# In the first block's two mixers, the z projection is put behind the values' projection inside the attention

## Chip, cores and metric

One core of one Trainium2 chip. The metric is device time in microseconds of one execution; the figure for the kernel before is the median of three runs. TensorE is PE here (its weight loads PEld), VectorE is DVE, ScalarE is ACT, GpSimd is POOL, and SyncE is SP, which issues the weight DMAs.

## What is computed

A sequence of 256 tokens of width 1024 goes through two blocks of two layers each, in fp32. A layer of the first block is a SwiGLU feed-forward, a hybrid mixer, and another feed-forward, each with a layer norm. Only the hybrid mixer matters here:

```python
def hybrid_mixer(x, w_in, b_in, ...):
    proj = x @ w_in + b_in
    (qa, ka, va, beta_raw, a_raw, za, qb, kb, vb, qc, kc, vc) = jnp.split(proj, split_at, axis=-1)
    o_a = gated_deltanet(qa, ka, va, beta_raw, a_raw, za, conv_w, a_log, dt_bias, gdn_norm_g)
    o_b = chunk_relpos_attention(qb, kb, vb, rel_bias)
    o_c = swa_sink_attention(qc, kc, vc, sinks)
    gates = jax.nn.sigmoid(x @ w_gate + b_gate).reshape(b, t, N_BRANCH, d)
    merged = (gates[:, :, 0] * (o_a @ w_br_a) + gates[:, :, 1] * (o_b @ w_br_b)
              + gates[:, :, 2] * (o_c @ w_br_c))
    return merged @ w_out

def gated_deltanet(qa, ka, va, beta_raw, a_raw, za, conv_w, a_log, dt_bias, norm_g):
    qkv = jax.nn.silu(causal_depthwise_conv(jnp.concatenate([qa, ka, va], -1), conv_w))
    ...
    beta = jax.nn.sigmoid(beta_raw)
    g = -jnp.exp(a_log) * jax.nn.softplus(a_raw + dt_bias)
    o = chunk_gated_delta_rule(q, k, v, g, beta)
    return o * lax.rsqrt(jnp.mean(o * o, -1, keepdims=True) + NORM_EPS) * norm_g * jax.nn.silu(z)
```

## The kernel before

**Products.** Every fp32 product is made of three matmuls on rounded parts: high times high, high times low, low times high (`mm3`, L444). The weights come from HBM in units of two k-tiles by 512 columns (SP, L2165). ACT rounds a unit to its high part (L922, "cut"), DVE subtracts to get its low part (L1266). Five units are cut ahead of their use.

**Order.** The order of all work is written out by one `Walk` that is replayed once per engine, so each engine runs its instructions in the order in which the Python code comes to them. Two things set it around the change. First, `attend` (L2518) advances nine attention items, one stage each, and after each round calls `fill(1)`. Second, `fill` (in `mixer1`) advances one generator of matrix work by one step of 12 small or 6 wide matmuls, and at every second step (at every step once the attention is over) pops one entry of a list `todo` of DVE and ACT work.

**The generator inside the attention** is `inputs_a`. It runs four parts of eight steps: the queries' columns (part 0), the keys' (part 1), then the part `None`, then the values' (part 2). Parts 0 to 2 write four PSUM banks of 256 columns each, which ACT empties (`conv_in`, L1015). The part `None` projects the delta rule's z together with beta and the decay inputs. It also uses four banks, DVE empties them in six instructions (`z_inputs`, L1399, L1400, L1402), and it appends four entries to `todo`: `decays_begin` (DVE L1460 to L1468, ACT L997), `decays_exp` (ACT L1004), `decays_log` (DVE L1475 to L1483), `decays` (DVE L1490 to L1501). These are 19 instructions on 8 columns each. Banks are handed out in the order in which they were given back (`bank`, L2290; `drop`, L2295).

**Behind the attention**, `gated()` is appended to `todo`: the convolution taps of the values (12 times DVE L1513), the silus of queries, keys and values (ACT L1028), the silu of z (ACT L1009). The generator becomes `others`: gate projection and branch output of the branches b and c, then the gate of a. After the eighth step of a gate projection DVE adds its bias (`gate`, L1679) and ACT takes the sigmoid (L1088). Once `todo` is empty, `delta` begins: its first matmuls are `gate_sums` (L607 to L611), `gd_rows` (L620), `gd_products` (L641) and `gd_turn` (L629). DVE's L1520 and ACT's L1033 empty the bank of `gate_sums`. DVE's L1587 gives LL, which PE needs at L651. `delta` is a long chain between PE, DVE, ACT and POOL, with `fill(2)` to `fill(4)` between its links:

```python
        state["every"] = 1
        todo.extend(gated())
        while not state["spent"]:
            fill(1)
...
        state["gen"], state["spent"] = others(), False
        fill(1)
        while todo:
            fill(1)
        ot = {}
        self.delta(l, fill, ot, done["b"] + done["c"])
```

Of the kernel before, what the change touches and what calls it, by code (L numbers as in the profile page):

```python
# [2221 lines left out]
class Walk:  # L2222
# [384 lines left out]
    def mixer1(self, l):  # L2607
# [36 lines left out]
        def convolve(j):  # L2644

            if j % 4 < 3:
                e.conv_first(l, j + 1)
            e.conv_taps(l, j)
# [5 lines left out]
                    lambda: e.conv_silu(l, 2), lambda: (e.z_gate(l, 0), e.z_gate(l, 1))]  # L2654

        def inputs_a():
            for part in (0, 1, None, 2):
                if part is None:
                    b0, b1 = [self.bank(), self.bank()], [self.bank(), self.bank()]
                    yield from self.rows(w_in, 8, 1536, [(0, 264, b0), (264, 256, b1)], self.x)  # L2660
                    for t in range(2):
                        e.z_inputs(l, t, b0[t], b1[t])
                        self.drop(b1[t], ("proj_v", (l, "z", t)))
                        self.drop(b0[t], ("proj_v", (l, "ba", t)))
                    todo.extend([lambda: e.decays_begin(l), lambda: e.decays_exp(l), lambda: e.decays_log(l), lambda: e.decays(l)])
                    continue
                bks = [self.bank() for _ in range(4)]
                yield from self.cols(w_in, 512 * part, 4, bks, self.x, steps=2)
                for j in range(4 * part, 4 * part + 4):
                    e.conv_in(l, j, bks[j % 4])  # L2670
                    self.drop(bks[j % 4], ("proj_a", (l, "q", j)))
                    if j % 4 == 1:
                        self.ahead(LEAD + 1)
                    if part < 2:
                        todo.append(lambda j=j: convolve(j))
                e.conv_first(l, 4 * part)

        state = {"gen": inputs_a(), "spent": False, "steps": 0, "every": 2}

        def fill(n):  # L2680
# [597 lines left out]
```

## Time and profile before

| | us |
|---|---|
| median of 3 runs | 2331.77 (2331.31 to 2331.85) |
| the profiled execution's own time | 2332.83 |
| its span in the trace | 2331.0 |
| PE busy | 2276.2 (98%) |
| DVE busy | 1485.0 (64%) |
| ACT busy | 1165.1 (50%) |
| POOL busy | 129.1 (6%) |
| granted PE clock, mean | 0.991 |

The two mixers of this kind run from about 320 to 565 us and from about 1165 to 1410 us of the span. A row of the timeline gives start, duration, engine, line, operation, output and inputs, and in brackets the idle time of the engine just before, with what ended it. Matmuls overlap, so a row's duration is longer than the distance to the next one.

### The profile page before, as it was taken

The page shows a single profiled execution, that of the slowest core. Times are in us where ns is not written, and L with a number is a line of the kernel's source. Part 1 is how long each engine was busy: PE and PEld are TensorE (multiplying, and loading weights), DVE is VectorE, ACT ScalarE, POOL GpSimd, SP SyncE. Part 2 cuts the span into 40 slices and gives each one's busy share as a digit, 9 for nine tenths or more (in the row PEclk, how much of TensorE's full clock was granted, in tenths as well). Part 3 has the DMA queues.
Part 4 walks back from the last instruction along what each step waited for, and adds up shares of the span by engine and source line. Part 5 has one row for each costly group of instructions (what it writes and reads, how often), then busy time and mean ns, then how long its engine had stood idle before and what let it go on. Part 6 is the DMA issues. An engine that isn't in the chain of part 4 may idle for free.

```text
span 2331.0 us, 33504 instructions
## 1 busy us (share of the span) xinstructions
PE 2276.2 (98%) x13839; PEld 1927.5 (83%) x13839; DVE 1485.0 (64%) x2139; ACT 1165.1 (50%) x1799; POOL 129.1 (6%) x197
## 2 busy tenths in 40 slices
PE   8999999999999999999999999999989999888999
PEld 7888798887888878888898877888878887766887
DVE  5665567857666556665667667666467664665663
ACT  5554346534555435553356344555344553545552
POOL 2100010120000000000100210000000000320000
PEclk9999999999999999999999999999999999999999
DMA  7856473445566556566553446566535665542663
GB/s 226 230 183 216 145 228 115 132 128 189 181 189 190 186 187 200 187 200 199 180 155 120 145 133 211 182 194 209 191 127 185 191 205 165 161 126 87 203 192 133
DMA packets 283560, 408.09 MB, mean 175 GB/s; under 512 B 13700, under 2 KB 170688, under 8 KB 283152
## 3 DMA queue, kind: packets, MB, share of 16 engines
q1 hardware_dynamic: 275600, 380.91, 51.4%
q0 software_dynamic: 7808, 25.04, 3.8%
q8 instruction: 109, 1.79, 0.3%
q14 instruction: 43, 0.35, 0.1%
HBM read 403.98 MB, written 1.91 MB: 174 GB/s over the span
## 4 chain that ended last, share of the span: by engine, by line
PE 85%; DVE 8%; ACT 4%; issue 1%; DMA 1%; POOL 0%; SPq 0%; DVEq 0%; ACTq 0%; POOLq 0%
PE PS L517 23%; PE PS L449 13%; PE PS L451 13%; PE PS L450 12%; PE PS L516 10%; DVE WL L1266 2%; PE PS L446 2%; PE PS L448 2%; PE PS L447 2%; PE PS L519 2%; PE PS L466 1%; ACT WH L922 1%; DVE QX L1513 1%; PE PS L661 0%; PE PS L677 0%
## 5 line engine op out<-in xcount | busy, mean ns | idle before, releaser
L1266 DVE TENSOR_TENSOR WL<-RW,WH 128x1024 fp32r<-128x1024 f32 (+2 forms) x732 | 870.8, 1220 | 315.8 <-ACT WH L922 312.2
L922 ACT ACTIVATE WH<-RW 128x1024 fp32r<-128x1024 f32 (+2 forms) x732 | 740.6, 1043 | 393.3 <-PE PS L451 220.9
L517 PE MATMUL PS<-XT,WH 128*128 128x512 f32 x2368 | 808.3, 394 | 0.0
L516 PE MATMUL PS<-XT,WL 128*128 128x256 f32 x2072 | 580.5, 280 | 0.0
L517 PEld LDWEIGHTS PS<-XT,WH 128*128 128x128 f32 x2368 | 425.0, 188 | 76.7
L516 PEld LDWEIGHTS PS<-XT,WL 128*128 128x128 f32 x2072 | 389.9, 188 | 13.3
L449 PE MATMUL PS<-WH,HTH 128*128 128x512 f32 x688 | 271.4, 394 | 0.0
L451 PE MATMUL PS<-WH,HTL 128*128 128x512 f32 x688 | 270.8, 394 | 0.0
L450 PE MATMUL PS<-WL,HTH 128*128 128x512 f32 x688 | 269.7, 392 | 0.0
L449 PE MATMUL PS<-WH,XT 128*128 128x512 f32 (+4 forms) x640 | 253.2, 396 | 8.0 <-DVE SX L1420 3.3
L451 PE MATMUL PS<-WH,XT 128*128 128x512 f32 (+4 forms) x640 | 243.0, 380 | 0.0
L450 PE MATMUL PS<-WL,XT 128*128 128x512 f32 (+4 forms) x640 | 242.5, 379 | 0.0
L446 PE MATMUL PS<-XT,WH 128*128 128x256 f32 x560 | 163.4, 292 | 2.4 <-DVE Z L1400 1.3
L449 PEld LDWEIGHTS PS<-WH,XT 128*128 128x128 f32 x640 | 123.7, 193 | 42.6 <-issue 9.9
L447 PE MATMUL PS<-XT,WL 128*128 128x256 f32 x560 | 157.6, 281 | 0.0
L448 PE MATMUL PS<-XT,WH 128*128 128x256 f32 x560 | 157.5, 281 | 0.0
L451 PEld LDWEIGHTS PS<-WH,HTL 128*128 128x128 f32 x688 | 129.1, 188 | 30.7
L1336 DVE TENSOR_TENSOR HM<-PS,HM 128x256 f32<-128x256 f32 x148 | 62.3, 421 | 144.3 <-ACT HM L952 144.3
L450 PEld LDWEIGHTS PS<-WL,HTH 128*128 128x128 f32 x688 | 129.1, 188 | 30.2
L449 PEld LDWEIGHTS PS<-WH,HTH 128*128 128x128 f32 x688 | 129.2, 188 | 28.9
L952 ACT ACTIVATE HM<-PS 128x256 f32<-128x256 f32 x148 | 57.0, 385 | 178.2 <-PE PS L517 174.0
L952 ACT ACTIVATE SG<-PS 128x256 f32<-128x256 f32 x148 | 57.1, 386 | 175.3 <-PE PS L517 174.6
(438 smaller groups left out, 2553.5 us busy)
## 6 DMA issues: line engine op xcount, KB each, us to landing
RW<-in_w_ff_in SPq DMA_DIRECT2D x256, 512.0 KB, 4.5
RW<-in_w_ff_out SPq DMA_DIRECT2D x128, 512.0 KB, 4.5
RW<-in_w_in SPq DMA_DIRECT2D x56, 512.0 KB, 4.5
RW<-in_w_gate SPq DMA_DIRECT2D x48, 512.0 KB, 4.3
RW<-in_ffn_gate SPq DMA_DIRECT2D x44, 512.0 KB, 4.6
RW<-in_ffn_up SPq DMA_DIRECT2D x44, 512.0 KB, 4.7
RW<-in_ffn_down SPq DMA_DIRECT2D x44, 512.0 KB, 4.5
RW<-in_w_out SPq DMA_DIRECT2D x16, 512.0 KB, 4.8
```

What stands on the lines that cost most here:

```text
L446: self.e.matmul(o, wh, xh, start=start, stop=False)
L447: self.e.matmul(o, wl, xh, start=False, stop=False)
L448: return self.e.matmul(o, wh, xl, start=False, stop=stop)
L449: self.e.matmul(o, xh, wh, start=start, stop=False)
L450: self.e.matmul(o, xh, wl, start=False, stop=False)
L451: return self.e.matmul(o, xl, wh, start=False, stop=stop)
L516: self.e.matmul(k.PS[:, b.n, 0:T], wl, k.XTH[:, kt, :], start=False, stop=False)
L517: ins = self.e.matmul(k.PS[:, b.n, :], wh, k.XT[:, kt, :], start=kt == 0, stop=kt == 7)
L922: self.e.activation(u.hi_out, raw, ACT.Copy).then_inc(*self.s["hi"].up(u.n))
L952: self.e.activation(f[2 + part][:, n, j * T:j * T + T], self.k.PS[:, b.n, 0:T], ACT.Copy).then_inc(*self.s["ffn_a"].up((seq, sl, n, part, j)))
L1266: self.e.tensor_tensor(u.lo_out, raw, u.hi_out.bitcast(F), ALU.subtract).then_inc(*self.s["lo"].up(u.n))
L1336: self.e.tensor_tensor(v, self.k.PS[:, b.n, T:2 * T], v, ALU.add).then_inc(*self.s["ffn_v"].up((seq, sl, n, part, j)))
```

## The change

One tuple is reordered, in `mixer1`:

```diff
         def inputs_a():
-            for part in (0, 1, None, 2):
+            for part in (0, 1, 2, None):
                 if part is None:
                     b0, b1 = [self.bank(), self.bank()], [self.bank(), self.bank()]
                     yield from self.rows(w_in, 8, 1536, [(0, 264, b0), (264, 256, b1)], self.x)
```

No operation is added or removed in the arithmetic. The weight units keep their sizes and their number; four units of 520 columns now come behind the four of the values. The four `decays` entries reach `todo` eight steps later.

On ACT, this is what stands between the silu of the values (first row) and the exponential of the decays (L1033), the piece of the difference in the first mixer; GT are the gates of branch b, WH the high parts of weights:

```order
 L1028 ACTIVATE QX<-QX 128x1024 [waits s_gdn_v]
+L1088 ACT_TABLE_LOAD
+L1088 ACTIVATE GT_82<-GT_82 128x512 [waits s_gate_v]
+L1088 ACTIVATE GT_83<-GT_83 128x512 [waits s_gate_v]
+L922 ACTIVATE WH<-RW 128x2x512 [waits s_mm,s_d_raw0]
+L922 ACTIVATE WH<-RW 128x2x512 [waits s_mm,s_d_raw1]
+L1009 ACT_TABLE_LOAD
 L1009 ACTIVATE Z<-Z 128x512 x2
 L1033 ACT_TABLE_LOAD
```

The gates of branch b and two cuts have moved in front of L1033, with two more table loads; ACT has four more rows in all, two per mixer.

On DVE, the same place before the change, from the last attention output (L1451) to the first instruction of `delta` (L1520); QX holds the convolved columns, WL the low parts:

```order
L1451 TENSOR_TENSOR Oc_90<-PS,Oc_89 128x128 [waits s_turn_hi]
L1266 TENSOR_TENSOR WL<-RW,WH 128x2x512 [waits s_hi] x2
L1513 SCALAR_TENSOR_TENSOR QX<-QP,VEC,QX 128x256 [waits s_proj_a]
L1513 SCALAR_TENSOR_TENSOR QX<-QP,VEC,QX 128x256 [waits s_gdn_v] x2
L1513 SCALAR_TENSOR_TENSOR QX<-QP,VEC,QX 128x256 [waits s_proj_a]
L1513 SCALAR_TENSOR_TENSOR QX<-QP,VEC,QX 128x256 [waits s_gdn_v] x2
L1513 SCALAR_TENSOR_TENSOR QX<-QP,VEC,QX 128x256 [waits s_proj_a]
L1513 SCALAR_TENSOR_TENSOR QX<-QP,VEC,QX 128x256 [waits s_gdn_v] x2
L1513 SCALAR_TENSOR_TENSOR QX<-QP,VEC,QX 128x256 [waits s_proj_a]
L1513 SCALAR_TENSOR_TENSOR QX<-QP,VEC,QX 128x256 [waits s_gdn_v] x2
L1266 TENSOR_TENSOR WL<-RW,WH 128x2x512 [waits s_hi] x2
L1520 COPY SX<-PS 128x8 [waits s_mm]
```

And with the change, from the second instruction of the first taps on:

```order
L1513 SCALAR_TENSOR_TENSOR QX<-QP,VEC,QX 128x256 [waits s_gdn_v] x2
L1266 TENSOR_TENSOR WL<-RW,WH 128x2x512 [waits s_hi] x2
L1513 SCALAR_TENSOR_TENSOR QX<-QP,VEC,QX 128x256 [waits s_proj_a]
L1513 SCALAR_TENSOR_TENSOR QX<-QP,VEC,QX 128x256 [waits s_gdn_v] x2
L1513 SCALAR_TENSOR_TENSOR QX<-QP,VEC,QX 128x256 [waits s_proj_a]
L1513 SCALAR_TENSOR_TENSOR QX<-QP,VEC,QX 128x256 [waits s_gdn_v] x2
L1513 SCALAR_TENSOR_TENSOR QX<-QP,VEC,QX 128x256 [waits s_proj_a]
L1513 SCALAR_TENSOR_TENSOR QX<-QP,VEC,QX 128x256 [waits s_gdn_v] x2
L1679 TENSOR_TENSOR GT_82<-PS,GB 128x512 [waits s_gdn_v,s_d_bias1,s_mm]
L1679 TENSOR_TENSOR GT_83<-PS,GB 128x512 [waits s_mm]
L1266 TENSOR_TENSOR WL<-RW,WH 128x2x512 [waits s_hi] x2
L1520 COPY SX<-PS 128x8 [waits s_mm]
```

L1679 has moved in front of L1520, and ahead of these rows now stand, behind the last attention output, the six instructions of `z_inputs`, two cuts and all 19 of the decays.

On PE, the end of the first group of `delta`'s matmuls before the change:

```order
L641 MATMUL PS<-QX 64x64 [waits s_proj_a]
L641 MATMUL PS<-QX 64x64 x15
L629 MATMUL PS<-CO,QX 128x128 [waits s_proj_a]
L629 MATMUL PS<-CO,QX 128x128 x3
L629 MATMUL PS<-CO,QX 128x128 [waits s_gdn_a,s_gdn_v]
L629 MATMUL PS<-CO,QX 128x128 x3
```

and with it:

```order
L641 MATMUL PS<-QX 64x64 [waits s_gate_v]
L641 MATMUL PS<-QX 64x64 x15
L629 MATMUL PS<-CO,QX 128x128 [waits s_gate_v]
L629 MATMUL PS<-CO,QX 128x128 x3
L629 MATMUL PS<-CO,QX 128x128 [waits s_gdn_a,s_gdn_v]
L629 MATMUL PS<-CO,QX 128x128 x3
```

The whole group stands three steps later in `others`: its first matmul (L607) followed 36 wide matmuls before and follows 54 now. The last wait of L629 is for the bank that L1520 (DVE) and L1033 (ACT) empty, before and now.

## Rows read from the trace of the kernel before

**Rows 1.** The page: PE's busy time and the chain that ended last.

```profile
PE 2276.2 (98%) x13839; PEld 1927.5 (83%) x13839; DVE 1485.0 (64%) x2139; ACT 1165.1 (50%) x1799; POOL 129.1 (6%) x197
...
PE 85%; DVE 8%; ACT 4%; issue 1%; DMA 1%; POOL 0%; SPq 0%; DVEq 0%; ACTq 0%; POOLq 0%
```

**Rows 2.** PE's waits, 340 to 560 us: who for whom, us, times, longest.

```profile
PE PS L585 <- DVE PP L1446: 2.0, 3, 0.9
PE PS L449 <- DVE SX L1420: 1.7, 1, 1.7
```

**Rows 3.** PE's timeline inside the attention, the stalls behind 380 us.

```profile
393.04 0.66 PE L585 MATMUL PS<-CO,PP 128*128 128x128 f32 x4 [0.38 <-DVE PP L1446]
...
398.05 0.28 PE L448 MATMUL PS<-XT,WH 128*128 128x256 f32 x1
398.97 0.39 PE L446 MATMUL PS<-XT,WH 128*128 128x256 f32 x1 [0.65 <-DVE Z L1400]
...
406.53 0.66 PE L585 MATMUL PS<-CO,PP 128*128 128x128 f32 x4 [0.71 <-DVE PP L1446]
```

**Rows 4.** PE's timeline from the first wide matmul of `others` to L651.

```profile
413.48 0.40 PE L449 MATMUL PS<-WH,XT 128*128 128x512 f32 x1
...
421.80 0.28 PE L607 MATMUL PS<-SX,CO 128*128 128x8 f32 x2
...
428.77 1.15 PE L641 MATMUL PS<-QX 128*64 128x64 f32 x32
429.85 0.33 PE L629 MATMUL PS<-CO,QX 128*128 128x128 f32 x1
...
438.12 1.15 PE L651 MATMUL PS<-CO,gLL 64*64 64x64 f32 x32 [0.25 <-DVE gLL L1587]
```

**Rows 5.** ACT's timeline, 416 to 437 us.

```profile
416.50 1.28 ACT L1028 ACT_TABLE_LOAD   x1
417.79 1.06 ACT L1028 ACTIVATE QX<-QX 128x1024 f32<-128x1024 f32 x1
...
423.72 1.06 ACT L1028 ACTIVATE QX<-QX 128x1024 f32<-128x1024 f32 x1 [0.83 <-DVE QX L1513]
424.69 1.14 ACT L1009 ACTIVATE Z<-Z 128x512 f32<-128x512 f32 x2
425.84 1.28 ACT L1033 ACT_TABLE_LOAD   x1
427.13 0.20 ACT L1033 ACTIVATE SX<-PS 128x32 f32<-128x32 f32 x1
...
432.16 1.23 ACT L1088 ACTIVATE GT<-GT 128x512 f32<-128x512 f32 x2 [0.22 <-DVE GT L1679]
433.30 2.96 ACT L922 ACTIVATE WH<-RW 128x1024 fp32r<-128x1024 f32 x3
```

**Rows 6.** DVE's timeline, 389 to 433 us.

```profile
389.62 2.36 DVE L1266 TENSOR_TENSOR WL<-RW,WH 128x1024 fp32r<-128x1024 f32 x2 [1.64 <-ACT WH L922]
...
398.17 0.41 DVE L1399 TENSOR_TENSOR Z<-PS,GB 128x256 f32<-128x256 f32 x1
...
399.57 0.15 DVE L1402 TENSOR_TENSOR SX<-PS,GB 128x8 f32<-128x8 f32 x1
...
409.95 1.16 DVE L1490 SCALAR_TENSOR_TENSOR SX<-SX 128x8 f32<-128x8 f32 x6
...
417.65 6.03 DVE L1513 SCALAR_TENSOR_TENSOR QX<-QP,VEC,QX 128x256 f32<-128x256 f32 x12
423.61 2.35 DVE L1266 TENSOR_TENSOR WL<-RW,WH 128x1024 fp32r<-128x1024 f32 x2
...
431.45 1.28 DVE L1679 TENSOR_TENSOR GT<-PS,GB 128x512 f32<-128x512 f32 x2
```

**Rows 7.** Windows of 10 us behind three stalls of PE; PEclk is the fifth figure.

```profile
379.28:389.28 10.00, 10.00 (x73) 9.36 (x74) 8.04 (x21) 4.72 (x16) 0.00 (x0) 0.86 0.32 105
1222.54:1232.54 10.00, 10.00 (x61) 9.27 (x62) 7.91 (x21) 3.28 (x12) 0.00 (x0) 0.70 0.34 105
2120.02:2130.02 10.00, 10.00 (x38) 8.05 (x39) 4.63 (x4) 4.82 (x5) 0.00 (x0) 0.86 0.35 107
```

## The prediction

> **What bounds the kernel now.** I read the page first. PE is busy 98% of the span, and 85% of the chain that ended last is PE [rows 1]. So nothing that DVE, ACT or the weight DMAs do costs time unless PE has to wait for it. The change gives PE the same matmuls in another order; its price is the difference between the waits of PE before and after, twice, because two mixers contain it. In PE's waits of the first mixer the rows to see are the three waits for PP and the one at the first z matmul [rows 2]. The timeline then dates those behind 380 us [rows 3], and the timelines of PE, ACT and DVE around the start of `delta` show how much room each had there [rows 4 to 6]. The second mixer repeats the pattern 844 us later.
>
> **Part 1: the projections change places inside the attention.** The z part and the values' part have the same number of matmuls of nearly the same width, so their PE time is exchanged one for one. The wait of 1.7 us ahead of the first z matmul is for a bank that the attention's DVE instruction L1420 gives back [rows 2]. It stays: the values' first matmul now needs the same bank, and ACT had emptied the other three by then.
>
> Three stalls behind it had z as their cause [rows 3]:
> - 0.38 us at 393.04. A row projection takes two units at once, so DVE waited 1.64 us for ACT and did two cuts in a row, 2.36 us, ahead of the softmax scale that PE needed [rows 6]. A column projection takes one unit in two steps. One cut of about 1.2 us moves behind the scale, and the stall goes.
> - 0.65 us at 398.97. The next projection needs the banks that DVE frees in six instructions from 398.17 to 399.7 [rows 6]. Now ACT frees them in four copies as soon as each column group ends, while z is next and needs them one at a time. It goes.
> - 0.71 us at 406.53. The same six instructions pushed the attention's DVE work back by 1.5 us. About 0.2 us of it stays, since two cuts now stand there in a pair.
>
> In start times each stall costs a little more than its idle figure, because the end of the matmul ahead overlaps it: 398.05 to 398.97 is 0.92 us where 0.12 us is usual, so 0.80 us. With the same for the others the three cost 2.2 us, and 0.2 us remain. **Gain: 2.0 us per mixer.**
>
> **Part 2: z and the decays arrive last.** Let 0 be the start of the first wide matmul of `others`, 413.48 before [rows 4]. PE's side: 36 wide matmuls take 8.32 us up to L607; now 18 more stand ahead of it, 4.3 us at 0.24 us each. From L607 to the L629 group are 8.05 us, and the four of it that wait last come 0.5 us on. PE wants the bank of `gate_sums` at 8.3 + 4.3 + 8.05 + 0.5 = 21.2.
>
> That bank is free when ACT's L1033 has read it, and ACT and DVE run in order. DVE: the second half of `z_inputs` to 1.0; the first exponential and the four small instructions to 2.0; two cuts, of which ACT does its half first, to 4.7; 15 more small ones at 1.16/6 = 0.19 us to 7.6; three taps, a quarter of 6.03 us, to 9.1; two cuts of 2.35 us to 11.4; nine taps, 4.5 us, to 15.9 [rows 6]. ACT behind the last tap: the values' silu 1.0 us, to 16.9; a table load 1.28, 18.2; two gate sigmoids 1.23, 19.4; two cuts 2.0, 21.4; a load 1.28, 22.7; z's silu 1.14, 23.8; a load 1.28, 25.1; the exponential 0.2, 25.3 [rows 5]. PE sees it at 25.4. **New stall: 25.4 - 21.2 = 4.2 us per mixer.** Before, the same exponential was done at 427.3 and the L629 group began at 429.85 [rows 4, 5], so there were 2.5 us of room and more.
>
> The two parts of this lateness are the 19 small instructions and half of `z_inputs`, which filled DVE's idle time inside the attention and now stand ahead of the taps, and the gate work of branch b with two more table loads, which now stand between the taps and the exponential. The gate's share comes from the order in which `todo` and `others` now interleave: `todo` holds four entries longer, so `others` has passed its eighth step.
>
> **Part 3: what a stall does to PE's clock.** Behind stalls of 1.67, 1.67 and 3.11 us the granted clock over 10 us was 0.86, 0.70 and 0.86 [rows 7]: part of that time ran at 1.2 GHz and the rest at 2.4 GHz. This cost (1 - 0.86) x 10 = 1.4 us twice and 3.0 us once. No stall as long as 4.2 us stands in the mixers before, so the price is bounded by these rows and by nothing at all if the clock holds. I take 1.4 us, which the longest of the three and one other show. **Cost: 1.4 us per mixer.**
>
> **Part 4: the rest.** L651 waited 0.25 us for LL [rows 4]. PE reaches it later than DVE does after the new stall, so this goes: gain 0.25 us. The other links of `delta` keep their distance in PE work and are shifted together with the stall; the gate work falls between other links. Its sigmoids and cuts, 3.2 us together [rows 5], may reach PE at one link: 0 to 1 us, taken as 0. The weight DMAs keep number and size, and PE waits for none of them in the mixers [rows 2]: 0. POOL's product on z starts about 12 us later and hides behind `delta`, which needs z at its end: 0. At the end of `others` three fewer steps are left to cover the last transposes; four remain, 5.8 us at 0.24 us per matmul: 0.
>
> **The sum**: -2.0 + 4.2 + 1.4 - 0.25 = 3.35 us per mixer, 6.7 for two. The profiled execution took 2332.83 us, so one like it would take 2339.5; the median is 1.06 us lower, so 2338.5. A measurement of this kernel can tell about 0.2%, 4.7 us, from no change, so this is slower by somewhat more than that.
>
> **A rule of the skill against this sum.** After the load at 416.50 the silu starts at 417.79, and after the one at 425.84 the exponential at 427.13: a table load holds ACT for 1.28 us and nothing more [rows 5]. The Trainium skill, ScalarE: Activation LUTs, What ACT_TABLE_LOAD costs, adds a drain of about 1.38 us to a load of about 1.28 us at every switch of set. By that page, three switches in the chain instead of loads alone would make the new stall 4.1 us longer in each mixer, an estimate. The rows show no such drain, and the sum goes by them.
>
> **Rivals.**
> - *The stall is about half as long.* ACT and DVE would have to gain 2 us over my count, for instance because PE's 54 wide matmuls run slower than 0.24 us beside more loads, or because attention work ends earlier. Then -2.0 + 2.1 + 0.9 - 0.25 = 0.8 us per mixer, 2333.3: within 0.2%. Against it: every term is an in-order queue with a duration from the trace. Chance 0.18.
> - *Faster.* If ACT's L1033 is done before PE's 21.2, only the gains of part 1 and of L651 are left: -2.25 us per mixer, 2327.3. The place is the last L629 group; it decides when the chain of part 2 is 4.2 us shorter, which would need ACT to be past the gates' sigmoids and both cuts before the last tap. The printed order puts them behind it. Chance 0.07.
> - *A longer stall.* If each of the three table switches held ACT for as long again as the load itself, 1.28 us, as some wait behind a switch would, the stall grows by 3.8 us: 2338.5 + 7.7 = 2346.2. The same end is reached if the clock takes its dearest row, 3.0 instead of 1.4 us, another link loses 1 us and the decays' round trips between ACT and DVE cost 1 us more: 2338.5 + 2 x 3.6 = 2345.7. The page named above is such a rule. The rows on loads speak against the first way, nothing against the second. Chance 0.15, of which 0.03 for the switches.
>
> **How the numbers follow.** Chance 0.60 for the forecast, which holds from 2336.5 to 2342.5. 2338.5 us is its time. Slower: 0.60 + 0.15 = 0.75. Same: 0.18. Faster: 0.07. The range goes from 2333.5, in the half-stall case, to 2347, behind the longer stall, and leaves out some 0.2: the faster case, the lower part of the half-stall case and the tail above.
>
> **What would show it.** PE's waits get a new row, L629 waiting for ACT's L1033 (or DVE's L1520), about 4 us long in each mixer and the longest there. The rows L446 on L1400 and most of L585 on L1446 behind 390 us vanish, the first wide matmul of `others` starts about 2 us earlier, near 411.5, and a window behind the stall has a clock near 0.86. Three table loads stand between the last silu of QX and L1033. The prediction is wrong if L629 does not wait, if its wait is for something earlier in the order, or if a later link of `delta` waits for several us.

## The result, and the profile after

The changed kernel takes 2341.94 us (median of 6 runs, 2340.47 to 2342.36); the kernel before takes 2331.77 us beside it (6 runs, 2331.31 to 2332.87). The ratio is 1.0042, with a 95% interval of 1.0031 to 1.0053: slower by 10.2 us. The profiled execution took 2341.11 us, its span is 2339.3 us. The forecast was slower by 6.7 us. The sign and the range held, and the size was a third too small. Among the experiments further down, one of the 11 executions of e5 took 2482.56 us at a mean granted clock of 0.848 and is left out of its ratio.

The page, beside [rows 1]:

```profile
PE 2276.9 (97%) x13839; PEld 1927.7 (82%) x13839; DVE 1489.1 (64%) x2139; ACT 1167.5 (50%) x1803; POOL 128.6 (5%) x197
...
PE 83%; DVE 9%; ACT 4%; issue 1%; DMA 1%; POOL 0%; SPq 0%; DVEq 0%; ACTq 0%; POOLq 0%
```

PE is busy for 0.7 us more than before, while the span is 8.3 us longer (2331.0 before). So in this pair of executions nearly all of the difference is idle time of PE. Busy time also holds what PE loses at a lower clock, and that differs from one execution to the next: the mean granted clock is 0.991 in both, although the changed kernel has two slow stretches of its own. PE's waits over the whole span of the changed kernel, in us, times and longest; these three rows are the ones that are new or larger in the two mixers (outside them, L449 on DVE's L1451 went from 3.1 to 3.9 us and L466 on L1329 from 7.6 to 5.0):

```profile
PE PS L629 <- ACT SX L1033: 7.9, 2, 3.9
...
PE PS L466 <- DVE MG L1706: 3.3, 4, 1.4
...
PE PS L672 <- ACT gPW L1055: 1.8, 2, 0.9
```

The first is the stall of part 2 of the prediction. The other two were taken as nothing in part 4. In [rows 2]'s stretch the waits of L446 on L1400 and of L585 behind 390 us are gone. PE's timeline of the first mixer, answering to [rows 4]:

```profile
411.15 0.39 PE L449 MATMUL PS<-WH,XT 128*128 128x512 f32 x1
...
431.68 0.66 PE L629 MATMUL PS<-CO,QX 128*128 128x128 f32 x4
436.27 0.79 PE L629 MATMUL PS<-CO,QX 128*128 128x128 f32 x4 [3.94 <-ACT SX L1033]
436.72 0.78 PE L449 MATMUL PS<-WH,Ob 128*128 128x512 f32 x1
...
445.33 1.15 PE L651 MATMUL PS<-CO,gLL 64*64 64x64 f32 x32
...
459.04 1.15 PE L672 MATMUL PS<-gPW,gBT 64*64 64x64 f32 x32 [0.93 <-ACT gPW L1055]
...
562.70 0.60 PE L466 MATMUL PS<-CO,MG 128*128 128x128 f32 x4
564.72 1.09 PE L466 MATMUL PS<-CO,MG 128*128 128x128 f32 x8 [1.43 <-DVE MG L1706]
```

`others` starts at 411.15 where it started at 413.48. The wide matmul behind the stall takes 0.78 us where one takes 0.40 elsewhere: PE came back at 1.2 GHz. ACT's timeline, answering to [rows 5], has the chain that ends at the stall:

```profile
426.74 1.06 ACT L1028 ACTIVATE QX<-QX 128x1024 f32<-128x1024 f32 x1 [5.82 <-DVE QX L1513]
427.82 1.28 ACT L1088 ACT_TABLE_LOAD   x1
429.11 1.15 ACT L1088 ACTIVATE GT<-GT 128x512 f32<-128x512 f32 x2
430.17 1.99 ACT L922 ACTIVATE WH<-RW 128x1024 fp32r<-128x1024 f32 x2
432.18 1.28 ACT L1009 ACT_TABLE_LOAD   x1
433.47 1.15 ACT L1009 ACTIVATE Z<-Z 128x512 f32<-128x512 f32 x2
434.64 1.28 ACT L1033 ACT_TABLE_LOAD   x1
435.93 0.20 ACT L1033 ACTIVATE SX<-PS 128x32 f32<-128x32 f32 x1
```

This is the order that the prediction wrote down: silu of the last columns, load, b's gate sigmoids, two cuts, load, z's silu, load, exponential, each starting where the one before ends. ACT idled 5.82 us for DVE ahead of it. DVE, answering to [rows 6]:

```profile
418.60 1.52 DVE L1513 SCALAR_TENSOR_TENSOR QX<-QP,VEC,QX 128x256 f32<-128x256 f32 x3
420.04 2.35 DVE L1266 TENSOR_TENSOR WL<-RW,WH 128x1024 fp32r<-128x1024 f32 x2
422.31 4.40 DVE L1513 SCALAR_TENSOR_TENSOR QX<-QP,VEC,QX 128x256 f32<-128x256 f32 x9
```

The values' taps (L1513), in [rows 6] one run from 417.65 on, stand here behind z, the decays and two cuts, and end at 426.7. In windows of 10 us behind two stalls, the new one and the 1.67 us one, the granted clock (the third figure from the end, here and in [rows 7]) is:

```profile
436.10:446.10 10.00, 9.82 (x60) 7.92 (x62) 9.45 (x19) 4.04 (x6) 2.08 (x2) 0.83 0.36 116
379.20:389.20 10.00, 10.00 (x75) 9.36 (x75) 8.06 (x21) 5.75 (x16) 0.00 (x0) 0.86 0.35 105
```

### The profile page after: what moved, and what is told of

Its sections match the earlier page's. It is cut to its first block, busy times and chain, and to the rows that moved or that the text cites. A ratio compares the mean times of both kernels' runs of the same rounds, so it can differ in the third digit from the quotient of the medians.

```text
span 2339.3 us, 33496 instructions
## 1 busy us (share of the span) xinstructions
PE 2276.9 (97%) x13839; PEld 1927.7 (82%) x13839; DVE 1489.1 (64%) x2139; ACT 1167.5 (50%) x1803; POOL 128.6 (5%) x197
## 4 chain that ended last, share of the span: by engine, by line
PE 83%; DVE 9%; ACT 4%; issue 1%; DMA 1%; POOL 0%; SPq 0%; DVEq 0%; ACTq 0%; POOLq 0%
PE PS L517 23%; PE PS L449 12%; PE PS L451 12%; PE PS L450 12%; PE PS L516 10%; DVE WL L1266 3%; PE PS L446 2%; PE PS L447 2%; PE PS L448 2%; PE PS L519 1%; ACT WH L922 1%; PE PS L466 1%; DVE QX L1513 1%; DMA RW<-in_w_in_odd 1%; ACT PP L978 0%
## 5 line engine op out<-in xcount | busy, mean ns | idle before, releaser
L1266 DVE TENSOR_TENSOR WL<-RW,WH 128x1024 fp32r<-128x1024 f32 (+1 forms) x732 | 871.6, 1222 | 315.5 <-ACT WH L922 313.3
L922 ACT ACTIVATE WH<-RW 128x1024 fp32r<-128x1024 f32 (+1 forms) x732 | 739.6, 1044 | 379.6 <-PE PS L451 208.3
L449 PE MATMUL PS<-WH,HTH 128*128 128x512 f32 x688 | 271.4, 394 | 0.0
L451 PE MATMUL PS<-WH,HTL 128*128 128x512 f32 x688 | 270.9, 394 | 0.0
L449 PE MATMUL PS<-WH,XT 128*128 128x512 f32 (+4 forms) x640 | 251.7, 393 | 5.0 <-DVE WL L1266 2.9
L451 PE MATMUL PS<-WH,XT 128*128 128x512 f32 (+4 forms) x640 | 241.7, 378 | 0.0
L446 PE MATMUL PS<-XT,WH 128*128 128x256 f32 x560 | 164.3, 293 | 4.8 <-DVE SX L1420 3.4
L449 PEld LDWEIGHTS PS<-WH,XT 128*128 128x128 f32 x640 | 122.2, 191 | 39.6 <-DVE XT L1277 9.0
L451 PEld LDWEIGHTS PS<-WH,HTL 128*128 128x128 f32 x688 | 129.1, 188 | 30.7
L449 PEld LDWEIGHTS PS<-WH,HTH 128*128 128x128 f32 x688 | 129.2, 188 | 28.9
```

What stands on the lines that cost most here:

```text
L446: self.e.matmul(o, wh, xh, start=start, stop=False)
L449: self.e.matmul(o, xh, wh, start=start, stop=False)
L451: return self.e.matmul(o, xl, wh, start=False, stop=stop)
L922: self.e.activation(u.hi_out, raw, ACT.Copy).then_inc(*self.s["hi"].up(u.n))
L1266: self.e.tensor_tensor(u.lo_out, raw, u.hi_out.bitcast(F), ALU.subtract).then_inc(*self.s["lo"].up(u.n))
```

## The experiments

The theory has two separate costs. One is a chain that runs in order through DVE and ACT and ends at L629. The other, which the prediction had not counted, is that `delta` starts three steps of `others` later, so that fewer steps are left to keep PE busy while later links are made ready. Nine kernels took these apart. Their times stand first; each was timed in 5 to 11 executions beside the kernel before on the same chip, and since the medians of that kernel were 2331.4 to 2332.3 us there, the ratios are the numbers to compare. The waits are those behind the first wide matmul of `others`; those under 0.5 us are left out, except where they are all there is or are spoken of below. "Start" is the number of steps of `others` ahead of `delta`, against the kernel before.

| kernel | start | us | ratio to before, 95% | waits of PE per mixer, us |
|---|---|---|---|---|
| the change | +3 | 2341.94 | 1.0042 (1.0031 to 1.0053) | L629 3.9, L672 0.9, L466 1.4 |
| e1_one_entry | 0 | 2333.65 | 1.0007 (0.9998 to 1.0015) | L651 3.1 |
| e2_taps_early | +1 | 2326.78 | 0.9979 (0.9970 to 0.9988) | none |
| e3_z_gate_late | +3 | 2338.98 | 1.0031 (1.0019 to 1.0042) | L629 1.7, L651 2.3, L466 1.4 |
| e4_delta_later | +3 | 2335.70 | 1.0018 (1.0009 to 1.0027) | L672 1.6, L466 1.4 |
| e5_taps_early_same_start | +3 | 2330.75 | 0.9994 (0.9985 to 1.0004) | L672 0.6, L466 1.4 |
| e6_before_taps_early | 0 | 2331.72 | 0.9998 (0.9989 to 1.0007) | as before |
| e7_one_entry_same_start | +3 | 2338.87 | 1.0032 (1.0020 to 1.0045) | L629 0.4, L651 2.3, L672 0.2 and 1.6, L466 1.4 |
| e8_taps_early_sooner_start | 0 | 2326.01 | 0.9976 (0.9968 to 0.9985) | L607 0.3 |
| e9_taps_early_two_sooner | -2 | 2349.15 | 1.0073 (1.0059 to 1.0087) | L672 2.4, L677 2.4, L729 1.3 |

### The later start alone: e4_delta_later

```diff
--- kernel before
@@ the mixer, ahead of delta
         while todo:
             fill(1)
+        fill(3)
         ot = {}
```

Expected:

> The kernel before, with its projection order, but three more steps of the other projection are issued ahead of the delta stage, which is the other thing that the change does by its longer list. Theory (the later start alone leaves VectorE's tail late, apart from any stall at L629): no wait of PE L629 on L1033, since the exponential ends at about 431.8 us where PE would now want it at 434.6; but PE L672 on L1055 about 0.9 us and PE L466 on L1706 about 1.4 us in each mixer, so 2333 to 2336 us. Rival (the later start costs nothing, as the prediction took it; all of the loss is the stall and the clock): 2331 to 2332.5 us, with L466 on L1706 at 0.2 us.

PE's waits, 300 to 600 us:

```profile
PE PS L466 <- DVE MG L1706: 1.7, 2, 1.4
PE PS L672 <- ACT gPW L1055: 1.6, 1, 1.6
```

L629 does not wait, and the time is 0.18% over the kernel before, 4.3 us, in the expected range; L672 waits longer than the 0.9 us expected. So the later start has a price of its own. One mixer's share can be read from landmarks. From the first wide matmul of `others` to the first L466 on MG it takes 145.60 us before (413.48 to 559.08) and 146.53 us here, and then PE waits on L1706 for 1.42 us instead of 0.20. That is 2.15 us per mixer, 4.3 for two, the measured difference.

The wait at L672 is one of order on ACT:

```profile
453.25 1.23 ACT L1088 ACTIVATE GT<-GT 128x512 f32<-128x512 f32 x2 [4.82 <-DVE GT L1679]
454.39 1.99 ACT L922 ACTIVATE WH<-RW 128x1024 fp32r<-128x1024 f32 x2
456.28 0.57 ACT L1055 ACTIVATE gPW<-PS 128x512 f32<-128x512 f32 x1
```

ACT idles 4.82 us at the gate sigmoids, since DVE reaches L1679 only at 452.54; then two cuts stand between them and the copy of gPW that PE needs. In the kernel before the same sigmoids fall one copy later: gPW's first copy ran at 447.94, ahead of them, and the second, behind them at 457.68, was done well before PE came for it at 459.85. The wait at L466 comes from DVE's end of the mixer. First DVE before, then in the changed kernel, from the cuts ahead of the last gate work L1694 on:

```profile
543.06 2.35 DVE L1266 TENSOR_TENSOR WL<-RW,WH 128x1024 fp32r<-128x1024 f32 x2
545.40 0.69 DVE L1694 TENSOR_TENSOR GTA<-PS,GB 128x512 f32<-128x512 f32 x1
548.17 0.69 DVE L1694 TENSOR_TENSOR GTA<-PS,GB 128x512 f32<-128x512 f32 x1 [2.07 <-PE PS L451]
...
559.28 0.69 DVE L1703 TENSOR_TENSOR GTA<-PS,GTA 128x512 f32<-128x512 f32 x1 [0.16 <-PE PS L451]
```

```profile
550.85 2.35 DVE L1266 TENSOR_TENSOR WL<-RW,WH 128x1024 fp32r<-128x1024 f32 x2
553.12 1.28 DVE L1694 TENSOR_TENSOR GTA<-PS,GB 128x512 f32<-128x512 f32 x2
...
565.30 0.69 DVE L1706 TENSOR_TENSOR MG<-MG,GTA 128x512 f32<-128x512 f32 x1
```

Before, DVE waits for PE 2.07 us at the second L1694 and 0.16 at the last L1703: it has room. After, both L1694 stand ready behind a pair of cuts, there is no wait for PE at either place, and PE waits instead. All five kernels with a start of +3 wait 1.4 us here, and the six others 0.2.

### The chain alone: e2_taps_early and e5_taps_early_same_start

e2 queues the values' taps inside the attention, as the other columns' taps are. Beside it, e5 adds two steps, which makes PE's order exactly that of the changed kernel.

```diff
--- changed kernel
@@ gated
-            taps = [lambda j=j: convolve(j) for j in range(8, 12)]
-            return [lambda: (e.conv_silu(l, 0), taps[0]()), lambda: (e.conv_silu(l, 1), taps[1]()), taps[2], taps[3],
+            return [lambda: e.conv_silu(l, 0), lambda: e.conv_silu(l, 1),
                     lambda: e.conv_silu(l, 2), lambda: (e.z_gate(l, 0), e.z_gate(l, 1))]
@@ inputs_a
-                    if part < 2:
-                        todo.append(lambda j=j: convolve(j))
+                    todo.append(lambda j=j: convolve(j))
@@ ahead of delta, e5 only
+        fill(2)
```

> The changed kernel, but the taps of the values' four tiles are queued inside the attention, right behind their projection, as the other parts' are, instead of behind the z inputs with the SiLUs. Theory (the stall at L629 is the end of an in-order chain: VectorE's taps of the values behind the decays, then ACT's SiLU of them, the z gate, two table loads and the exponential): the first link is about 6 us earlier, so the stall of PE L629 on ACT SX L1033 goes or falls under 1 us; the early gain of 2 us per mixer stays unless the taps make a VectorE wait inside the attention; the tail wait at L466 on L1706 (1.4 us) stays, since the delta stage still starts three steps later. Time 2331 to 2335 us. Rival (the stall is the table loads of ACT and would stand wherever the taps are): L629 waits over 3 us and the time is 2340 to 2343.

> The run with the values' taps inside the attention, with two more steps of the other projection ahead of the delta stage, so that TensorE's instructions stand in exactly the order of the changed kernel; only the order on VectorE and ScalarE differs from it. Theory (two separate costs: the in-order chain in front of L1033, and the later start of the delta stage): no wait of PE L629 on L1033, but PE L466 on L1706 at 1.4 us and PE L672 on L1055 at 1 to 1.6 us in each mixer, as in the run that only starts the delta stage later: 4 to 5 us over the run with the earlier taps (2326.8), so 2330 to 2332.5 us. Rival (the late tail is a consequence of the stall, or the earlier taps themselves relieve VectorE's tail): L466 waits 0.2 us and the time is 2326 to 2328.

e2 takes 2326.78 us, under both kernels and under the interval expected for it. Its expectation was wrong in one point: the shorter list made `delta` start two steps sooner than in the changed kernel, not at the same place, so the wait on L1706 went too. That mixed the two costs, and e5 separates them: its time and its wait at L466 are as expected, and L672 waits 0.6 us where 1 to 1.6 was. PE's timeline of e5:

```profile
412.11 0.39 PE L449 MATMUL PS<-WH,XT 128*128 128x512 f32 x1
...
440.58 1.15 PE L651 MATMUL PS<-CO,gLL 64*64 64x64 f32 x32
...
557.62 0.60 PE L466 MATMUL PS<-CO,MG 128*128 128x128 f32 x4
559.64 0.55 PE L466 MATMUL PS<-CO,MG 128*128 128x128 f32 x3 [1.42 <-DVE MG L1706]
```

From the first wide matmul to the first L466 on MG are 145.51 us; the changed kernel, with the same instructions of PE in the same order, needs 151.55 (411.15 to 562.70). The place of the taps is thus worth 6.0 us per mixer, 12 for two. The ratios say 1.0042 - 0.9994 = 0.48%, 11.2 us; inside the attention the earlier taps cost e5 a new wait of 0.4 us at L585, and its stretches ahead of `others` are 0.55 and 0.31 us longer than those of the changed kernel. From the first L629 to L651 are 7.94 us in e5 and 13.65 in the changed kernel. Of the 5.7 us between them 3.94 are the stall and 1.8 the slower stretch behind it. In the 10 us behind L629 the clock of e5 stayed at 1.00:

```profile
432.60:442.60 10.00, 10.00 (x107) 8.33 (x103) 9.29 (x19) 2.92 (x4) 1.04 (x1) 1.00 0.32 110
```

e5 against e2 repeats the price of the later start: 0.9994 - 0.9979 = 0.15%, 3.5 us, which the waits at L466 and L672 cover, 2 x 1.2 and 2 x 0.6.

### Is it the taps or the order: e6_before_taps_early

The same edit on the kernel before, with the last two taps as one entry, so that PE's order is exactly that of the kernel before.

```diff
--- kernel before
@@ gated
-            taps = [lambda j=j: convolve(j) for j in range(8, 12)]
...
@@ inputs_a
-                    if part < 2:
-                        todo.append(lambda j=j: convolve(j))
+                    if j < 10:
+                        todo.append(lambda j=j: convolve(j))
+                    elif j == 11:
+                        todo.append(lambda: (convolve(10), convolve(11)))
```

> The kernel before, with z in its old place, but the values' taps queued inside the attention, with the same steps ahead of the delta stage: TensorE's order is exactly that of the kernel before. Theory (what the run with the earlier taps gained over the kernel before comes from the order of the projections, the stalls of 0.4 to 0.7 us inside the attention that vanish): PE L446 on Z L1400 0.6 us and PE L585 on L1446 2.0 us stay, and the time is that of the kernel before, 2330 to 2332.5 us. Rival (the gain comes from the taps' place alone): 2326 to 2328.5 us.

2331.72 us, a ratio of 0.9998: no change, and L585 waits 2.0 us and L446 on L1400 0.7 as before. So the taps' place gains nothing by itself. e8 further down starts `delta` where e6 does and has the new order of the projections; its ratio of 0.9976 against 0.9998 is what that order gains. From the 1.67 us wait at 379 us to the first wide matmul of `others`, the kernels with the old order (before, e4, e6; two mixers each) take 32.9 to 35.7 us, 34.6 in the mean, and the eight kernels with the new order 31.1 to 33.8, 32.4 in the mean. That is 2.1 us less per mixer. It isn't the luck of the clock: mixers with the same granted clock behind that wait differ by as much, 34.3 and 32.3 us in the mean at 0.83 to 0.86, 35.7 and 33.6 at 0.69 to 0.70, 32.9 and 31.1 at 1.00.

### Shortening the chain by its links: e3_z_gate_late, e1_one_entry, e7_one_entry_same_start

e3 moves z's silu behind the exponential. e1 makes the four entries of the decays one, so that `delta` starts as before. e7 is e1 with three steps added, which gives PE exactly the order of the changed kernel.

```diff
--- changed kernel, e3
@@ gated
-                    lambda: e.conv_silu(l, 2), lambda: (e.z_gate(l, 0), e.z_gate(l, 1))]
+                    lambda: e.conv_silu(l, 2), lambda: None]
@@ delta
+        e.z_gate(l, 0)
+        e.z_gate(l, 1)
         ub, wb = [self.bank(), self.bank()], [self.bank(), self.bank()]
         e.gd_apply(l, ub, wb)
--- changed kernel, e1 and e7
@@ inputs_a
-                    todo.extend([lambda: e.decays_begin(l), lambda: e.decays_exp(l), lambda: e.decays_log(l), lambda: e.decays(l)])
+                    todo.append(lambda: (e.decays_begin(l), e.decays_exp(l), e.decays_log(l), e.decays(l)))
@@ ahead of delta, e7 only
+        fill(3)
```

> The changed kernel, but the SiLU of z (L1088, with its table load) is not issued ahead of the delta stage's exponential, but behind it, ahead of the delta rule's application. Theory: ACT's chain ahead of L1033 loses one table load's 1.28 us at most and 2.3 us of SiLUs with their reads, so L629's stall falls from 3.94 to 1.5 to 2.5 us; the later SiLU brings two table loads to a place where ACT has room, though it may delay one SX exponential there. Tail wait at L466 on L1706 stays at about 1.4 us. Time 2337 to 2340 us. Rival (VectorE's taps alone set the stall): L629 still waits 3.5 us or more, and the time is that of the change or above, 2341 to 2344.

> The changed kernel, but the four parts of the decays are one entry of the list, so that the delta stage begins three steps of the other projection earlier, as in the kernel before, with the projection order of the change kept. Theory (two costs: a stall of PE at L629 on ACT's exponential, and a late tail of VectorE because the delta stage starts later): in each mixer the stall of PE L629 on ACT SX L1033 stays but is shorter, about 2.5 us where the changed kernel has 3.94, since the gates of b's rows go behind that exponential; the wait on the bank of b's gates (PE L672 on ACT gPW L1055, 0.93) goes; the wait of PE L466 on VectorE's L1706 (1.42) goes back to 0.2. So 3 to 4 us less per two mixers than 2 x (1.4 + 0.9 + 1.2) = 7 at most: 2335 to 2338 us, against 2341.9 for the change and 2331.8 for the kernel before. Rival (only the stall and the clock behind it cost anything): the tail wait stays at 1.4 us or the 7 us of other links come back whatever the start of the delta stage; then 2339 to 2341.

> The changed kernel with the decays as one entry and three more steps ahead of the delta stage: TensorE's order is exactly that of the changed kernel, and ScalarE's differs in little more than that z's SiLU stands ahead of b's gates, so that one table load of 1.28 us less lies in front of L1033, and that the taps come some 2.3 us earlier on VectorE. Theory (the chain in front of L1033 is in order, and each microsecond taken out of it comes off the stall): the stall of 3.94 us falls to 0 to 1.0 us; L651 on L1587 waits at most 1.5 us; the tail wait L466 on L1706 stays at 1.4 and L672 on L1055 at 0.9 to 1.6. Time 2332 to 2336 us. Rival (it is b's gates ahead of L1033 that set the stall, wherever the taps and z are): L629 waits over 2.5 us and the time is 2338 to 2342.

(The first expectation names L1088 for z's silu, which is the line of the gates' sigmoids; z's silu is L1009, 1.15 us for both halves.) The stall at L629 shrank about by what was taken out of the chain: e3, without z's silu and the load of 1.28 us in front of it, has 1.72 us instead of 3.94; e7 has 0.37, as expected. But a wait that no expectation had at this size came up behind it. PE's timeline of e3, then the two instructions that empty the bank of `gate_sums` there and DVE's L1587:

```profile
435.60 0.63 PE L629 MATMUL PS<-CO,QX 128*128 128x128 f32 x4 [1.72 <-ACT SX L1033]
...
445.48 0.73 PE L651 MATMUL PS<-CO,gLL 64*64 64x64 f32 x17 [2.34 <-DVE gLL L1587]
```

```profile
435.07 0.16 DVE L1520 COPY SX<-PS 128x8 f32<-128x8 f32 x1
...
444.74 0.69 DVE L1587 TENSOR_TENSOR gLL<-PS,gDS 128x512 f32<-128x512 f32 x1
```

```profile
435.26 0.20 ACT L1033 ACTIVATE SX<-PS 128x32 f32<-128x32 f32 x1 [0.25 <-DVE SX L1520]
```

And PE's of e1:

```profile
438.88 0.51 PE L651 MATMUL PS<-CO,gLL 64*64 64x64 f32 x10 [3.07 <-DVE gLL L1587]
```

The chain does not end at L629, and it forks ahead of it. Behind the last tap, ACT's gate sigmoids and two cuts release DVE's two cuts, and L1520 stands behind those. In e3 and e7 ACT idles 0.25 us for L1520 before the exponential: the branch through DVE is now the longer one, and what is left of the stall stands on the gates and the cuts, no longer on a table load. From L1520 on DVE goes through its list with a single wait of 0.4 us, for ACT's L1040: the reductions, L1687 and two cuts stand ahead of L1587, and from L1520 to L651 it takes 10.4 us in e3 and in e7 (435.07 to 445.48, 432.53 to 442.94). PE needs 7.94 us from the first L629 to L651. L1520 just in time for L629 is therefore too late for L651. In the changed kernel this was hidden: without its stall PE would have come to L651 at 431.68 + 7.94 = 439.6 and waited until 444.66 for L1587, some 5.0 us, an estimate. So of the 5.7 us between e5 and the changed kernel, taking away the stall at L629 alone would have brought back some 0.7.

So e3 (2338.98) came out only 3 us under the changed kernel, inside its expected range, and e7 at 2338.87 missed its expectation of 2332 to 2336 by 3 us. In e1 `delta` starts as before, but L1520 comes 15.3 us behind the first wide matmul instead of 12.4. L629 had the room for these 2.9 us and does not wait, against the expectation; L651 had none, as its 0.25 us in [rows 4] had shown already, and waits 3.07. e1 ended 1.4 us under its expectation of 2335 to 2338.

### How far a sooner start goes: e8 and e9

```diff
--- e2
@@ inputs_a, e8
-                    todo.extend([lambda: e.decays_begin(l), lambda: e.decays_exp(l), lambda: e.decays_log(l), lambda: e.decays(l)])
+                    todo.extend([lambda: (e.decays_begin(l), e.decays_exp(l)), lambda: e.decays_log(l), lambda: e.decays(l)])
@@ inputs_a, e9
+                    todo.append(lambda: (e.decays_begin(l), e.decays_exp(l), e.decays_log(l), e.decays(l)))
```

> The run with the earlier taps, with the first two parts of the decays as one entry, so that the delta stage begins one step sooner, as in the kernel before. Theory: VectorE's tail is then as early as in the kernel before, which was early enough already (0.2 us at L466), and PE L651 may come to wait on L1587, for whose chain there is one step (about 1.4 us) less cover, 0 to 1 us in each mixer: 2326.5 to 2329 us, no better than the run with the earlier taps. Rival (a sooner start goes on gaining): under 2326 us.

> The run with the earlier taps and all four parts of the decays as one entry, so that the delta stage begins two steps of the other projection sooner than in the kernel before. Theory (the later start costs because VectorE's and ScalarE's late links lose cover; once the tail is early enough a sooner start buys nothing more and begins to lay bare the links in front of the delta stage): L466 on L1706 stays at 0.2 us, PE L607 waits on L1501 for 0.3 to 1.5 us and L651 on L1587 for 0 to 1.5 us in each mixer, so 2326 to 2330 us, not under the run that starts with the kernel before's steps (2326.0). Rival (each step sooner gains its 1 to 2 us): 2321 to 2324 us.

e8 takes 2326.01 us, 0.5 us under its expectation; L651 does not wait, and L607 waits 0.3 us for DVE's L1501. Its interval overlaps that of e2, so a step sooner than e2 makes no difference that these executions can tell. Both beat both kernels. e9, two steps sooner still, takes 2349.15 us, the slowest of all, and neither theory nor rival had that. The waits are not at L607 or L651 but at three later links:

```profile
459.11 0.48 PE L672 MATMUL PS<-gPW,gBT 64*64 64x64 f32 x6 [2.42 <-ACT gPW L1055]
...
490.99 0.51 PE L677 MATMUL PS<-gBT,gPW 64*64 64x64 f32 x10 [2.42 <-ACT gPW L1055]
...
525.85 0.37 PE L729 MATMUL PS<-VN,gKDC 64*128 64x128 f32 x1 [1.26 <-DVE VN L1623]
```

ACT's timeline ahead of the first has the pattern of e4, stronger:

```profile
456.05 0.63 ACT L1088 ACTIVATE GT<-GT 128x512 f32<-128x512 f32 x1 [3.44 <-DVE GT L1679]
456.59 1.99 ACT L922 ACTIVATE WH<-RW 128x1024 fp32r<-128x1024 f32 x2
458.48 0.57 ACT L1055 ACTIVATE gPW<-PS 128x512 f32<-128x512 f32 x1
```

Here DVE waits 3.38 us for PE's gate matmul (L451), ACT 3.44 for DVE, and the copy of gPW stands behind both, so PE waits for itself around the ring. The price is not monotone in the start: L672 waits 2.4 us at -2, not at all in the kernels with 0 and +1, and 0 to 1.6 at +3. That this depends on where the gates' steps fall against the copies is read from the two timelines; no run moved the gates' steps alone. The three waits are 6.1 us per mixer of the 10.2 and 11.7 us by which e9's two mixers exceed those of the kernel before between the two landmarks. Three more waits of 0.3 us at L672 and the clock are nearly all of the rest: the 10 us behind the first and the third wait were granted 0.83 and 0.83 in the first mixer and 0.84 and 0.66 in the second, which is 3.4 and 5.0 us.

## Why the prediction was right, and where it was off

Per mixer, from the traces:

- **Part 1, -2.0 us.** Right. The three stalls vanished as described, the 1.67 us one stayed, and the means above give -2.1.
- **Part 2, +4.2 us.** Right in mechanism, place and order of the links; the wait was 3.94 us in both mixers. e2 and e5 show that the stall goes when the first link is moved, and in e3 and e7 it shrank by what was taken out of the chain. That the stall belongs to the chain is thus shown; e6 shows that the taps' place behind the attention costs nothing where z is early. What part 2 did not have is the fork: L651 hung on the same cuts through L1520, and would have waited some 5 us by itself. After the load at 434.64 the exponential starts at 435.93, 1.29 us later: the drain that the Trainium skill adds (ScalarE: Activation LUTs, What ACT_TABLE_LOAD costs) did not appear in this chain of three switches, and the rival built on it fell.
- **Part 3, +1.4 us.** Measured as 1.8 in both mixers, against e5. The granted clock was 0.83 behind the stall in both, where 0.86 was taken; that it fell both times could not be known, as the last section shows. Nor would all of the 1.8 us be gone with a clock that holds: in the changed kernel DVE's L1587 ended at 444.66, 0.67 us ahead of PE. A PE at full clock would have come 1.8 us sooner and waited some 1.1 us for it, an estimate.
- **Part 4** is the step that failed, in two of its zeros. The gates' sigmoids and cuts "may reach PE at one link: 0 to 1 us, taken as 0": the link was L672, with 0.93 us, the top of its bounds. "At the end of `others` three fewer steps are left to cover the last transposes; four remain", taken as 0: DVE was late at L466, with 1.43 and 0.24 us where 0.20 had stood. The argument counted the steps that remain on PE, and did not ask what DVE still owes at that point. e4 shows both with no stall ahead of them, so they come from the start alone and not from the stall. The 0.25 us of L651 went, as said, because the stall and the slow stretch together were longer than the lateness of L1587.

The sum of the mixer: -2.1 in the attention; +5.9 from the first wide matmul to the first L466 on MG (151.55 against 145.60 us), in which the stall, the stretch behind it and L672 are +6.4 net of L651 and some -0.4 came back at L706 and near it; +1.5 at the last transposes. That is 5.3 us, 10.6 for two, against 10.2 measured and 6.7 forecast.

Of the rivals, the half-length stall did not come, nor the faster case. The longer stall gave 2345.7 to 2346.2 by ways of which one was met in part: another link did lose 1 us.

## What to carry to other kernels

When a list of deferred work grows by some entries, two things move: the work in it, and everything that waits for the list to be empty. Price both, and for the second follow every later link to its end on each in-order engine, asking what that engine still owes when the consumer arrives. A stall can hide a later link that is late by the same chain: shortening the path to the first alone lets the next one wait in its place (L651 here). And the start of an interleaved stage has a phase against the periodic work of other engines; move it both ways before calling one place good, since from e8's start two steps sooner cost 23 us and one step later nothing that could be measured.

## What the runs showed of the hardware that was not expected

The same wait was followed by different clocks. PE waits 1.67 us in e2 and 1.68 us in e8 at the second mixer's first z or value matmul, with the same order of PE's instructions around it, and the 10 us behind it are granted 0.70 and 1.00 (third figure from the end). First e2, then e8:

```profile
1220.60:1230.60 10.00, 10.00 (x62) 9.27 (x63) 8.01 (x21) 4.29 (x12) 0.00 (x0) 0.70 0.35 105
```

```profile
1222.00:1232.00 10.00, 9.99 (x86) 9.06 (x88) 8.91 (x22) 6.50 (x18) 0.00 (x0) 1.00 0.36 105
```

PE worked on 62 matmuls in the one window and on 86 in the other. The stretch up to `others` took 33.75 us in e2 and 31.07 in e8, so such a wait costs 0 to 3 us in a single execution beyond its own length. Over all the kernels with the new order that stretch takes 33.5 to 33.8 us where the clock was 0.69 or 0.70, 32.0 to 32.6 at 0.83 to 0.86, and 31.1 at 1.00. This is most of the scatter among the means above, and a reason to compare the stretches of several executions before a microsecond is put down to an edit.

The same is seen inside one execution. In both mixers of e1, L651 waits 3.07 or 3.08 us, and this is what follows:

```profile
438.88:448.88 10.00, 10.00 (x96) 8.42 (x96) 9.93 (x13) 3.31 (x4) 1.99 (x1) 0.83 0.55 178
1284.69:1294.69 10.00, 10.00 (x129) 8.51 (x130) 9.93 (x13) 3.50 (x5) 1.43 (x2) 1.00 0.52 170
```

From the first wide matmul to the first L466 on MG the first mixer took 150.09 us and the second 148.56. e7 has the same pair, 0.83 and 1.00 behind its 2.3 us wait at L651, but there the two mixers took 149.57 and 149.50 us: the faster PE then waited 1.63 us at L672, the slower one 0.19. A lost clock costs nothing where a later link would have held PE anyway. What decides whether the clock falls was not tried.
